# Up stages of a two-layer encoder: VectorE makes three of the seven lo parts of each weight pair

## What is computed

```python
def conv_ffn(h, w_in, conv_w, conv_b, w_out):
    u = h @ w_in                      # 1024 x 1024 by 1024 x 5632
    u = conv_general_dilated(u, ...)  # causal, depthwise, width 3
    gate, val = jnp.split(u, 2, axis=-1)
    return (jax.nn.gelu(gate, approximate=True) * val) @ w_out
```

## Time and profile before

| what | value |
|---|---|
| median of three runs | 2338.32 us (2337.2 to 2340.23) |
| the profiled execution, its own time | 2339.69 us |
| its span in the profile | 2337.9 us |
| PE busy | 2264.2 us, 97% |
| VectorE, ScalarE, GpSimd busy | 75%, 51%, 39% |
| pairs of layer 0 | about 786 to 1152 us of the span |
| pairs of layer 1 | about 1751 to 2115 us |

### The profile page before, as it was taken

One profiled execution on the slowest core, in us unless ns is written; L12 is line 12 of the kernel. 1 busy time (PEld: TensorE's weight loads), 2 busy tenths in 40 slices (PEclk: granted clock), 3 DMA queues, 4 the chain that ended last, 5 costly groups with the idle time before them and its releaser, 6 DMA issues. The chain is left out here.

```text
span 2337.9 us, 31779 instructions
## 1 busy us (share of the span) xinstructions
PE 2264.2 (97%) x11307; PEld 1909.4 (82%) x11307; DVE 1755.1 (75%) x2650; ACT 1189.2 (51%) x1956; POOL 915.9 (39%) x778
## 2 busy tenths in 40 slices
PE   6999999999999999999999989999999999999998
PEld 5778778999888788888888868888887888887886
DVE  4786787865545788888899757656577888889986
ACT  5558876766543343444444644455534333444454
POOL 2223334511012777887500012142167788771000
PEclk9999998999999999999999999899999999999999
DMA  5111100000332122222473532311322222228435
GB/s 154 44 39 46 37 28 28 19 1 1 127 110 71 63 82 81 84 91 88 165 250 110 173 133 68 93 41 46 99 64 82 81 87 85 82 81 288 152 118 189
DMA packets 190359, 215.17 MB, mean 92 GB/s; under 512 B 15508, under 2 KB 136692, under 8 KB 190204
## 3 DMA queue, kind: packets, MB, share of 16 engines
q1 hardware_dynamic: 185452, 195.84, 26.4%
q10 hardware_dynamic: 4752, 17.30, 1.8%
HBM read 170.77 MB, written 39.98 MB: 90 GB/s over the span
## 5 line engine op out<-in xcount | busy, mean ns | idle before, releaser
L123 PE MATMUL trunk_ps<-l_bhi,l_ahi 128*128 128x512 f32 x528 | 206.6, 391 | 4.4 <-DVE l_blo L2906 4.4
L123 PE MATMUL trunk_ps<-l_bhi,l_alo 128*128 128x512 f32 x528 | 205.6, 389 | 0.0
L123 PE MATMUL trunk_ps<-l_blo,l_ahi 128*128 128x512 f32 x528 | 205.4, 389 | 0.0
L123 PE MATMUL trunk_ps<-l_t_hi,l_s_hi 128*128 128x512 f32 x456 | 178.3, 391 | 3.6 <-POOL l_s_lo L2529 3.6
L123 PE MATMUL trunk_ps<-l_t_hi,l_s_lo 128*128 128x512 f32 x456 | 178.0, 390 | 0.0
L123 PE MATMUL trunk_ps<-l_t_lo,l_s_hi 128*128 128x512 f32 x456 | 178.0, 390 | 0.0
L2529 POOL TENSOR_TENSOR l_s_lo<-l_raw,l_s_hi 128x512 fp32r<-128x512 f32 x90 | 159.0, 1775 | 42.8 <-ACT l_s_hi L2435 42.8
L2311 ACT ACTIVATE l_ahi<-l_a 128x512 fp32r<-128x512 f32 x132 | 83.1, 630 | 135.3 <-PE trunk_ps L123 128.3
L216 POOL TENSOR_TENSOR wring_w_lo<-wring_raw,wring_w_hi 128x256 fp32r<-128x256 f32 x88 | 77.6, 913 | 180.8 <-ACT wring_w_hi L211 180.8
L2529 POOL TENSOR_TENSOR l_s_lo<-l_w_sum,l_s_hi 128x512 fp32r<-128x512 f32 x76 | 120.0, 1581 | 48.1 <-ACT l_s_hi L2435 48.1
L123 PEld LDWEIGHTS trunk_ps<-l_bhi,l_ahi 128*128 128x128 f32 x528 | 99.1, 188 | 28.9 <-DVE l_alo L2903 5.9
(11 more groups left out here) (466 smaller groups left out, 6776.4 us busy)
## 6 DMA issues: line engine op xcount, KB each, us to landing
l_draw<-in_ffn_w_out SPq DMA_DIRECT2D x154, 256.0 KB, 2.7
l_raw<-in_ffn_w_in SPq DMA_DIRECT2D x48, 512.0 KB, 4.6
gated_dram<-l_gate_out SPq DMA_DIRECT2D x44, 512.0 KB, 2.6
l_a<-gated_dram SPq DMA_DIRECT2D x88, 256.0 KB, 4.0
wring_raw<-in_even_w_in SPq DMA_DIRECT2D x20, 512.0 KB, 3.9
l_raw_g<-in_ffn_w_in SPq DMA_DIRECT2D x20, 512.0 KB, 3.8
l_raw_v<-in_ffn_w_in SPq DMA_DIRECT2D x20, 512.0 KB, 4.9
l_wt<-in_ffn_w_out SPq DMA_DIRECT2D x22, 256.0 KB, 5.9
```

The lines of the kernel that those rows point to most:

```text
L123: mm = pe.matmul(o, w, m, start=a, stop=z, skip_group_check=onto)
```

## The change

VectorE takes the lo parts of S1, S3 and A22 in every pair (`weight_lo`); GpSimd keeps those of A11, S2, A12 and S4. The three count on a semaphore of their own, `s_lo_taken`, and whoever waited for `s_lo_done` waits for one or for both. The arithmetic is the same.

```diff
+        LO_BY_POOL, LO_BY_DVE = (A11, S2, A12, S4), (S1, S3, A22)
+        def wait_lo(eng, m):
+            r, q = divmod(m, 7)
+            if q in LO_BY_DVE:
+                eng.wait_ge(s_lo_taken, 3 * r + LO_BY_DVE.index(q) + 1)
+            else:
+                eng.wait_ge(s_lo_done, 4 * r + LO_BY_POOL.index(q) + 1)
+        def wait_pairs(eng, n):
+            eng.wait_ge(s_lo_done, 4 * n)
+            eng.wait_ge(s_lo_taken, 3 * n)
...
                 def load_pair(r):
                     if r >= 2:
-                        sp.wait_ge(s_lo_done, 7 * (r - 1))
+                        wait_pairs(sp, r - 1)
...
-                    for q in (S2, S1, S3, A12):
+                    for q in (S2, A12):
                         s_lo_part(7 * r + q)
                     pool.wait_ge(s2_done, r + 1)
-                    pool.wait_ge(s_lo_done, 7 * r + A12 + 1)
+                    wait_lo(pool, 7 * r + A12)
                     pool.tensor_tensor(weight_of(r, S4), weight_of(r, A12), w_sum[1][:], ALU.subtract).then_inc(s4_done, 1)
-                    for q in (S4, A22):
-                        s_lo_part(7 * r + q)
+                    s_lo_part(7 * r + S4)
...
-                    pe.wait_ge(s_lo_done, m + 1)
+                    wait_lo(pe, m)
...
                     if r:
-                        dve.wait_ge(s_lo_done, 7 * (r - 1) + S1 + 1)
+                        wait_lo(dve, 7 * (r - 1) + S1)
...
+                def weight_lo(r, q):
+                    if r >= NS:
+                        return
+                    m = 7 * r + q
+                    dve.wait_ge(s_hi_done, m + 1)
+                    dve.tensor_tensor(s_lo[m % NW][:], weight_of(r, q), s_hi[m % NW][:].bitcast(F32), ALU.subtract).then_inc(s_lo_taken, 1)
...
                 taps("v", 1)
+                weight_lo(0, S1)
+                weight_lo(0, S3)
                 gate(1)
...
                 gate(2)
                 dve.wait_ge(t4_lo_done, QUARTER)
+                weight_lo(0, A22)
                 weight_sums(1)
...
                     merge(r)
                     last_corner(r)
+                    weight_lo(r + 1, S1)
+                    weight_lo(r + 1, S3)
                     weight_sums(r + 2)
                     first_corner(r)
                     upper_corner(r)
                     taps("g", i)
                     lower_corner(r)
+                    weight_lo(r + 1, A22)
```

More of the change, by code:

```diff
@@ L1995, in trunk_stage @@
         s1_done, s2_done, s3_done, s4_done = (st.sem(f"s{i}_done") for i in (1, 2, 3, 4))
-        s_hi_done, s_lo_done, product_done = st.sem("s_hi_done"), st.sem("s_lo_done"), st.sem("product_done")
+        s_hi_done, s_lo_done, s_lo_taken, product_done = st.sem("s_hi_done"), st.sem("s_lo_done"), st.sem("s_lo_taken"), st.sem("product_done")
         first_done, merge_done, part_done, third_done, c11_done, c12_done, c21_done, c22_done = (
@@ L2160, in load_row @@
                     if q < NR:
-                        sp.wait_ge(s_lo_done, 7 * (NS - 1))
+                        wait_pairs(sp, NS - 1)
                     else:
```

## The result

| | median | runs | ratio to before, 95% interval |
|---|---|---|---|
| before | 2339.05 us | 2337.20 to 2340.23, 4 runs | 1 |
| after | 2364.66 us | 2359.25 to 2367.98, 4 runs | 1.0108 [1.0087, 1.0129] |

The change costs 25.6 us. The forecast was 2344.3, with a range up to 2364; the result lies 0.7 us above that range, at the figure of the first rival (2364). The profiled execution of after took 2363.26 us, 23.6 more than that of before. It reached the pairs of layer 0 2.7 us earlier than before's did, by a difference that arose in the first 280 us, where nothing was changed.

The account below looks back on a forecast made before the run. TensorE was taken to bound the kernel, with VectorE's round 0.08 us behind. 2 x 2.55 (start) + 1.8 (clock) - 0.9 (down stages) = +6.0 us, or 2344.3 us on the median; own range 2341 to 2350, eight in ten 2340 to 2364.

Parts of the forecast that it names:

- the first rival: In the loop GpSimd wins the tie at the port, the gate still waits, round 19.65 us; 2364 us, chance 0.22.
- What bounds the kernel: TensorE is busy 97%; VectorE's round of 18.96 us has 0.08 us to spare against TensorE's 19.04.
- Part 1, the start: Start of a layer's pairs: new TensorE wait of 4.7 us at A22 of pair 0, old 1.79 gone; +2.55 us a layer.
- The clock: TensorE's clock falls behind the new wait in each layer, layer 0 having paid already; +1.8 us, bounds 0 and 3.5.
- Part 2: A round of the pair loop: five steps bring VectorE's round to 19.0 us, still within TensorE's 19.04.
- step 2, the tie: In the loop VectorE's gate (846.15) meets GpSimd's A12 lo part (846.14); VectorE taken as first, gate 1.23 us: -0.92 us.
- 1. first v tap: Start of a round: GpSimd's sum S2 is ready earlier, the tap finds the port free, 1.28 for 1.58: -0.3 us.
- 3. lo parts of S1 and S3: Behind last_corner on VectorE: two added steps of 0.60 us, both finding the port free; +1.2 us a round.
- 4. the sums: VectorE's sums wait once for GpSimd, for the lo part of S4 instead of L2550; +0.07 us a round.
- 5. lo part of A22: Behind lower_corner it falls into VectorE's 1.31 us wait for ScalarE's tap; 0, up to +0.7 us.
- Part 3, the down stages: TensorE comes later relative to VectorE, so some of its 1.2 and 2.7 us waits go; -0.9 us, between 0 and -3.9.
- The threshold: In the loop, VectorE's round decides only once over 19.15 us; each tenth above costs 3.2 us.

Follow-up runs that it names:

- start_only: Changed kernel, but VectorE makes the lo parts of S1, S3 and A22 for pair 0 only, GpSimd all others; 2343.26 us, ratio to before 1.0017.
- same_moment: Changed kernel, but GpSimd's lo part of A12 also waits for VectorE's second v tap, which releases the gate; 2345.91 us, ratio to before 1.0027.
- before_later: Kernel before, with the two sums of weights for pair r + 2 moved behind the upper corner; 2332.05 us, ratio to before 0.9966.
- dve_s1s3: Changed kernel, but VectorE makes only the lo parts of S1 and S3, for pairs 1 to 17, GpSimd all others; 2357.20 us, ratio to before 1.0077.
- dve_a22: Changed kernel, but VectorE makes only the lo part of A22, for pairs 1 to 17, GpSimd all others; 2334.17 us, ratio to before 0.9976.
- best_before: Kernel before, with pair 1's sums ahead of tile 2's v taps and ScalarE's first product copy waiting for the token pieces; 2336.89 us, ratio 0.9995.
- a22_best: Kernel before, with VectorE making A22's lo part from pair 1, pair 1's sums ahead of tile 2's v taps, later sums behind upper corner; 2328.77 us, 0.9955.
- a12_early: Changed kernel, but ScalarE makes the hi part of A12 ahead of those of S1 and S3 from pair 1 on; 2355.75 us, ratio to before 1.0068.

## Why the prediction was wrong, step by step

**What bounds the kernel** was right: TensorE, with VectorE's round 0.08 us behind it as the number that decides. So was the rule for the port: one waits until the other has ended, less 0.15 us.

**Part 1, the start**: right. The new wait is 4.45 and 4.56 us for 4.7, the 1.8 us wait is gone, and in start_only TensorE is 2.5 us later by pair 2 of layer 0, for the 2.55 forecast.

**The clock**: right. It fell behind each of the two long waits, and in layer 1 of start_only TensorE is 4.1 us late by pair 2, 1.6 more than in layer 0, for the 1.8 forecast.

**Part 2** holds the step that failed, **step 2, the tie**, with its term of -0.92 us. I took VectorE as the first, from one row in which it was served although it had started 0.01 us later. GpSimd started 0.05 us ahead and won in all 34 rounds in which the two met. Counted from the start of the v taps, the gate starts at 3.61 us, for 3.60 forecast, but GpSimd at 3.55, for 3.59: ScalarE's hi part of A12 ends 0.72 us earlier than before, for 0.70, and two more hundredths came from rounding. So 0.04 us in the working decided it. The terms, each a difference between starts of the same two operations, in us a round:

| step | forecast | same_moment (VectorE first) | after (GpSimd first) |
|---|---|---|---|
| 1. first v tap | -0.30 | -0.29 | -0.30 |
| 2. gate | -0.92 | -0.93 | +0.17 |
| 3. lo parts of S1 and S3 | +1.20 | +1.21 | +1.75 |
| 4. the sums | +0.07 | +0.12 | -0.98 |
| 5. lo part of A22 | 0 | 0 | 0 |
| round, from 18.97 | 19.0 | 19.08 | 19.62 (the terms are good to 0.01) |

The middle column is the prediction with its tie won, and of the terms of the round none but the tie's is wrong by more than 0.05 us. same_moment measures +6.2 us against its set's before, where the sum said +6.0. That closeness is in part luck. The interval goes from 3.0 to 9.6. The down stages give back far more than was forecast when VectorE keeps up (Part 3), and here a round of 19.08, which was to cost nothing, takes that away again. The right column is the first rival, which said 19.65 (its own terms add up to 19.61) and 2364.

The Trainium skill, page "SBUF — State Buffer", section "Who interferes with whom", says that issue order decides who is blocked. By after (GpSimd 0.05 us ahead) and same_moment (0.01 behind), the trace agrees. The row at 851.15 that I set against it is no single case. VectorE's first sum and GpSimd's L2550 meet like this in 32 rounds of before. VectorE is served first in 28 of them, with GpSimd's start between 0.012 us ahead and 0.004 behind; GpSimd is served first in four, with its start 0.012 to 0.017 us ahead. One of the four, VectorE's row and then GpSimd's:

```profile
908.23 1.82 DVE L2828 TENSOR_TENSOR l_w_sum<-l_raw 128x512 f32<-128x512 f32 x1
```

```profile
908.21 1.28 POOL L2550 TENSOR_TENSOR l_raw_g<-l_raw_g,l_w_sum 128x512 f32<-128x512 f32 x1
```

So a lead of 0.01 us in the profile does not give the port to GpSimd, and one of 0.05 does. The row was read rightly for a tie; it was no tie.

The chance was wrong too. Two starts 0.01 us apart by sums of terms that are each good to some hundredths are no forecast of an order, so 0.50 against 0.22 had little to rest on. And the range ended at the rival's central figure: it had to reach past it, since the rival's own terms were as uncertain as the forecast's.

**Part 3, the down stages**: the sign was right only for a VectorE that keeps up. In after they wait 2.6 and 2.4 us where it was 1.2 and 2.7, so nothing came back. In start_only they wait 0.8 and 0.7, 2.4 less for both, and TensorE regains 3.6 us there, where I took 0.9. The prediction also put part of these waits down to DMAs; before_later, whose one edit is in VectorE's order, removes them all.

**The threshold** of 19.15 us was wrong: dve_s1s3 (19.38) pays from 18.97 on, and same_moment (19.08), which has the start of start_only, waits 4.1 us in the down stages where start_only waits 1.5.

## What to carry to other kernels

Where two engines share a port, write down for each meeting which of them is ready first and by how much; if it is less than the error of the sum, both orders are outcomes of the same weight. Look for what the loser queues behind: here a gate on the bounding chain lost 1.1 us a round to an operation that had 10 us to spare, and one wait that holds that operation back by 0.06 us took off 19 us. And before work is moved onto an engine that has 0.08 us a round to spare, make room on it: moving two sums into an idle 1.3 us made even the unchanged kernel 0.34% faster.

## What the runs showed of the hardware

- The order at the shared port goes by hundredths of a microsecond. GpSimd ahead by 0.05 us: it takes 1.29, VectorE's gate 2.31. GpSimd behind by 0.01 us: the gate takes 1.23, GpSimd 2.37. In between, VectorE's first sum and GpSimd's L2550 meet 128 times in before, start_only, dve_a22 and best_before; GpSimd is served first in five of them, all with its start 0.012 to 0.017 us ahead. With another operation the line can lie elsewhere: in a22_best GpSimd was served ahead of a tap of VectorE twice, with starts 0.00 and 0.01 us apart.
- The one that waits gets the port some 0.15 us before the other's operation ends by the trace, and an operation of GpSimd that becomes ready during one of VectorE's goes ahead of VectorE's next (924.09 against 924.32 in a12_early).
- In some traces VectorE starts one operation of layer 0 0.44 us after the one ahead of it (same_moment at 945.40), with nothing in the profile to release it. What that is these runs don't tell. It was enough to turn the order at the port for that round.
- A wait of 4.4 to 4.6 us of TensorE brought its clock to 1.2 GHz behind it in after and in start_only, in both layers (means of 0.61 to 0.79 over the stretches behind). The wait of 1.8 us did so in layer 0 of before and not in layer 1.
